# 54 of 66 gate/up pairs as seven block products of 256 tokens each

## What is computed

```python
h = rms_norm(x, norm_ffn_pre[i])
gu = jnp.einsum('bsd,df->bsf', h, w_gu[i])
f = jnp.einsum('bsf,fd->bsd', jax.nn.silu(gu[..., :D_FF]) * gu[..., D_FF:], w_down[i])
x = x + rms_norm(f, norm_ffn_post[i])
```

## Time and profile before

| | |
|---|---|
| runs (3) | 2337.39 us median, 2334.93 to 2341.15 |
| the profiled execution's span, first to last instruction | 2331.0 us |
| mean granted TensorE clock | 0.986 |
| busy: TensorE, VectorE, ScalarE, GpSimd | 2232.4, 1015.4, 885.3, 1024.3 us |
| matmuls | 14692 |

### The profile page before, as it was taken

One profiled execution on the slowest core, in us unless ns is written; L12 is line 12 of the kernel. 1 busy time (PEld: TensorE's weight loads), 2 busy tenths in 40 slices (PEclk: granted clock), 3 DMA queues, 4 the chain that ended last, 5 costly groups with the idle time before them and its releaser, 6 DMA issues.

```text
span 2331.0 us, 36126 instructions
## 1 busy us (share of the span) xinstructions
PE 2232.4 (96%) x14692; PEld 1838.9 (79%) x14692; DVE 1015.4 (44%) x1655; ACT 885.3 (38%) x1506; POOL 1024.3 (44%) x605
## 2 busy tenths in 40 slices
PE   7999999999999999999998999999968999999998
PEld 6867888888986688888886888867757778888888
DVE  6264522211346654222116798726674455322212
ACT  5264532322424654323225222353535445322322
POOL 4423544444543155444446444433430465444443
PEclk9999999999999999999999999999989999999999
DMA  6601343333352023333333333332201432333332
GB/s 176 150 25 37 90 118 93 98 101 100 79 127 73 2 64 100 100 93 95 107 86 109 103 100 93 111 100 78 82 3 40 146 84 79 109 97 93 94 99 70
DMA packets 386295, 209.88 MB, mean 90 GB/s; under 512 B 36927, under 2 KB 378663, under 8 KB 385875
## 3 DMA queue, kind: packets, MB, share of 16 engines
q1 hardware_dynamic: 383011, 196.68, 29.7%
q0 software_dynamic: 2448, 9.70, 1.1%
q10 hardware_dynamic: 672, 1.18, 0.1%
HBM read 196.65 MB, written 12.41 MB: 90 GB/s over the span
## 4 chain that ended last, share of the span: by engine, by line
PE 81%; issue 7%; POOL 6%; DVE 4%; ACT 2%; DMA 0%; ACTq 0%; POOLq 0%; DVEq 0%
PE ps L2372 23%; PE ps L2374 23%; PE ps L2373 23%; POOL w_lo L835 3%; PE ps L2582 2%; PE ps L2567 2%; PE ps L2557 2%; POOL x_res L902 1%; PE ps L2545 1%; POOL u_b L932 0%; PE ps L2952 0%; PE ps L2835 0%; PE ps L2946 0%; PE ps L2445 0%; POOL scratch_z L943 0%
## 5 line engine op out<-in xcount | busy, mean ns | idle before, releaser
L835 POOL TENSOR_TENSOR w_lo<-raw,w_hi 128x1024 fp32r<-128x1024 f32 (+2 forms) x344 | 822.8, 2396 | 886.4 <-ACT w_hi L1026 881.4
L2372 PE MATMUL ps<-h_hi,w_hi 128*128 128x512 f32 (+1 forms) x2112 | 816.6, 387 | 22.2 <-DVE h_lo L1714 4.5
L2373 PE MATMUL ps<-h_hi,w_lo 128*128 128x512 f32 (+1 forms) x2112 | 804.7, 381 | 0.0
L2374 PE MATMUL ps<-h_lo,w_hi 128*128 128x512 f32 (+1 forms) x2112 | 804.6, 381 | 0.0
L1026 ACT ACTIVATE w_hi<-raw 128x1024 fp32r<-128x1024 f32 (+1 forms) x344 | 358.1, 1042 | 1111.9 <-PE ps L2374 1100.1
L2372 PEld LDWEIGHTS ps<-h_hi,w_hi 128*128 128x128 f32 x2112 | 399.0, 189 | 114.9 <-issue 32.6
L2374 PEld LDWEIGHTS ps<-h_lo,w_hi 128*128 128x128 f32 x2112 | 399.1, 189 | 76.6
L2373 PEld LDWEIGHTS ps<-h_hi,w_lo 128*128 128x128 f32 x2112 | 399.4, 189 | 74.8 <-issue 1.2
L2372 PE MATMUL ps<-hid_hi,w_hi 128*128 128x512 f32 (+1 forms) x616 | 221.8, 360 | 0.0
L2374 PE MATMUL ps<-hid_lo,w_hi 128*128 128x512 f32 (+1 forms) x616 | 220.9, 359 | 0.0
L2373 PE MATMUL ps<-hid_hi,w_lo 128*128 128x512 f32 (+1 forms) x616 | 220.9, 359 | 0.0
(11 more groups left out here) (360 smaller groups left out, 2457.8 us busy)
## 6 DMA issues: line engine op xcount, KB each, us to landing
raw<-in_w_gu SPq DMA_DIRECT2D x88, 512.0 KB, 3.7
raw<-in_w_in SPq DMA_DIRECT2D x56, 512.0 KB, 3.7
raw<-in_w_down SPq DMA_DIRECT2D x32, 448.0 KB, 3.5
raw<-in_ffn_w_gate SPq DMA_DIRECT2D x22, 512.0 KB, 3.7
raw<-in_ffn_w_up SPq DMA_DIRECT2D x22, 512.0 KB, 3.7
raw<-in_w_in_b SPq DMA_DIRECT2D x20, 512.0 KB, 3.7
raw<-in_w_down SPq DMA_DIRECT2D x16, 512.0 KB, 3.7
raw<-in_w_out SPq DMA_DIRECT2D x16, 512.0 KB, 3.8
```

The costliest lines, as they stand in the source:

```text
L835: nc.gpsimd.tensor_tensor(lo[:, k0:, :], src[:, k0:, :], hi[:, k0:, :].bitcast(f32), ALU.subtract).then_inc(lo_done, 1)
L2372: nc.tensor.matmul(bank, wh[:, k, :], ah[:, part], start=first, stop=False)
L2373: nc.tensor.matmul(bank, wl[:, k, :], ah[:, part], start=False, stop=False)
L2374: return nc.tensor.matmul(bank, wh[:, k, :], al[:, part], start=False, stop=end)
```

## The change

Pairs 0, 1, 2 and 21 stay as they are (CLASSIC). The other 18 pairs (SEVEN) of each FFN are computed by a block scheme. Take the gate and the up as two rows, the inputs as two halves of four chunks and the tokens as two halves of 256: a product of 2x2 blocks by 2x2 blocks. It has eight block products of 4 chunks x 256 tokens; the new form has seven. For these the kernel forms
- of the activations, once per FFN, four sums of 4 chunks x 256 tokens (`t_sum`, VectorE, `gated_sums`, eight instructions inside the joint and eight behind the first gate), each with a high part by ScalarE (`t_hi`) and a low part (`t_lo`, two by VectorE, two by GpSimd); `later_left` holds one scaled quarter (ScalarE);
- of the weights, per pair, S1, S2 and S4 by VectorE into two PSUM banks (`w_sums`, `w_last_sum`), with high parts by ScalarE and low parts by VectorE (`low_of_sum`), and S3 by GpSimd (`w_diff`). The plain quarters A11, A12 and A22 are split by ScalarE and GpSimd (`high_part`, `low_parts`).

TensorE does the products in the order A11, A12, S2, S1, S3, S4, A22, each 4 chunks x 3 matmuls of 256 tokens, and accumulates several into one bank. What a bank holds in between is copied by ScalarE (`kept`) and added by VectorE: C11, C22, C12 in the code are the results gate/first half, up/second half, gate/second half, and C21 is up/first half. The `w_hi` and `w_lo` slots are now handed out by half slots, and `used` counts pieces. `hid` is kept whole for all 22 tiles; the high and low parts of tiles 3 to 21 come after the last block product, apart from three. Some semaphores are merged with others. The cut diff, its indentation of twelve shortened:

```diff
+HALF = TOK // 2
+CLASSIC = (0, 1, 2, KF - 1)
+SEVEN = tuple(f for f in range(KF) if f not in CLASSIC)
+A11, A12, S2, S1, S3, S4, A22 = range(7)
+T_OF = {S1: 0, S2: 1, S3: 2, A22: 3}
...
+def low_parts(p):
+    s = seven_at[p]
+    diff = w_diff[:, s % 2, :, :]
...
+    nc.gpsimd.tensor_tensor(diff, raw[:, raw_slot[p], 0:4, :], raw[:, raw_slot[p + 1], 0:4, :], ALU.subtract
+                            ).then_inc(sg["w_by_pool"], 1)
+    for j, src in ((A11, raw[:, raw_slot[p], 0:4, :]), (A12, raw[:, raw_slot[p], 4:8, :]), (S3, diff),
+                   (A22, raw[:, raw_slot[p + 1], 4:8, :])):
+        pool.wait_ge(hi_done, place_of[p, j] + 1)
+        pool.wait_ge(used, split_after[p, j])
+        nc.gpsimd.tensor_tensor(split_of(w_lo, p, j), src, split_of(w_hi, p, j).bitcast(f32), ALU.subtract
+                                ).then_inc(lo_done, 1)
...
+def gated_lows(tag):
+    split_lo(L["gu" + tag].p0 + 4)
+    pool.wait_ge(sg["t_steps"], 18 * int(tag) + 8)
+    split_lo(L["gu" + tag].p0 + 5)
+    for m, i in enumerate((T_OF[S3], T_OF[A22])):
+        pool.wait_ge(sg["t_by_act"], 8 * int(tag) + 7 + m)
+        nc.gpsimd.tensor_tensor(t_lo[:, i, :, :], t_sum[:, i, :, :], t_hi[:, i, :, :].bitcast(f32), ALU.subtract
+                                ).then_inc(sg["t_low_by_pool"], 1)
+    split_lo(L["gu" + tag].p1)
...
+def high_part(p, j):
+    s = seven_at[p]
...
+    act.wait_ge(used, split_after[p, j])
+    nc.scalar.activation(split_of(w_hi, p, j), src, ACT.Copy).then_inc(hi_done, 1)
+    if j == A22:
+        nxt[0] += 2
...
+    if after in ("gu0", "gu1", "gu2"):
+        for c in range(4):
+            nc.scalar.activation(beside_x(name, later_left[:, c, :]), x_part(name, c, cols_of(1)), ACT.Copy,
+                                 scale=gain(c)).then_inc(sg["t_by_act"], 1)
...
 def ffn(tag):
-    for i, b in groups("gu" + tag):
-        f = i // 2
...
+    for i in range(4):
+        act.wait_ge(sg["t_steps"], 18 * no + 4 * (i + 1))
+        k = (T_OF[S1], T_OF[S2], T_OF[S3], T_OF[A22])[i]
+        nc.scalar.activation(t_hi[:, k, :, :], t_sum[:, k, :, :], ACT.Copy).then_inc(sg["t_by_act"], 1)
+    first = l.p0 + 2 * SEVEN[0]
+    ahead = {2: (A11, A12), 3: (S2, S1), 4: (S3, S4), 5: (A22,)}
+    last = l.p0 + 2 * SEVEN[-1]
+    for i in range(6):
+        split_hi(min(l.p0 + i + 3, first))
+        act.wait_ge(used, upto(l.p0 + i + 1))
         if i % 2 == 0:
-            n["ffn"] += 1
-            freed(act, L["gu" + tag].g0 + i)
-            nc.scalar.activation(silu[:, f % 2, :], silu[:, f % 2, :], ACT.Silu).then_inc(sg["silu_ready"], 1)
-            if i == 0:
-                split_hi(L["gu" + tag].p0 + 6)
-        else:
-            act.wait_ge(sg["hid_ready"], n["ffn"])
-            nc.scalar.activation(hid_hi[:, f, :], hid[:, f % 2, :], ACT.Copy).then_inc(sg["hid_hi_ready"], 1)
+            freed(act, l.g0 + i)
+            silu_of(i // 2)
+        split_hi(min(l.p0 + i + 4, first))
+        for j in ahead.get(i, ()):
+            high_part(first, j)
+        if i % 2:
+            hid_high(i // 2)
+    high_part(first + 2, A11)
+    for f in SEVEN:
+        p = l.p0 + 2 * f
+        s = seven_at[p]
+        x, y, z, _ = seven_banks(no, s)
+        for j in range(PRODUCTS):
+            if j == A11:
+                keep(0, p, j, x, C11)
+            if j == S2:
+                keep(1, p, j, x, C12)
+            if j == S1:
+                keep(2, p, j, z, C22)
+            if j == A22:
+                gated_to(act, s, GATE)
+                silu_of(f)
+            if j != A22 and p != last:
+                high_part(p + 2, j + 1)
+            if j == A22 and p + 2 < last:
+                high_part(p + 4, A11)
+            if p == last and j in (S1, A22):
+                split_hi(p + 3 + (j == A22))
+    for f in range(3, 6):
+        hid_high(f)
+    act.wait_ge(used, place_of[last, A22] + 1)
+    split_hi(l.p1 + 1)
+    for f in range(6, 10):
+        hid_high(f)
+    split_hi(l.p1 + 2)
+    freed(act, l.g0 + 6)
+    silu_of(KF - 1)
+    for f in range(10, KF):
+        hid_high(f)
+    n["hid"] += KF
...
+def gated_sums(no, name, gain, second):
+    def left(c, half):
+        return x_part(name, c, cols_of(half))
+    def t_of(j, c):
+        return beside_x(name, t_sum[:, T_OF[j], c, :])
+    for c in () if second else range(4):
+        dve.wait_ge(sg["t_by_act"], 8 * no + c + 1)
+        nc.vector.scalar_tensor_tensor(t_of(S1, c), left(c, 0), gain(c), beside_x(name, later_left[:, c, :]),
+                                       ALU.mult, ALU.subtract).then_inc(sg["t_steps"], 1)
...
+    def w_sums(p):
+        s = seven_at[p]
+        a, b = (chunks(bank) for bank in sum_banks(p))
+        if p == l.p0 + 2 * SEVEN[0]:
+            freed(dve, l.g0 + 2)
+            freed(dve, l.g0 + 3)
+        else:
+            weights_to(dve, s - 1, LOW_S4)
+        nc.vector.scalar_tensor_tensor(a, raw_half(p + 1, 0), -1.0, raw_half(p + 1, 1), ALU.mult, ALU.subtract
+                                       ).then_inc(sg["w_by_dve"], 1)
+        weights_to(dve, s, SUM_S1)
+        nc.vector.scalar_tensor_tensor(b, a, -1.0, raw_half(p, 0), ALU.mult, ALU.subtract
+                                       ).then_inc(sg["w_by_dve"], 1)
+    def low_of_sum(p, j):
+        bank = sum_banks(p)[j == S2]
+        dve.wait_ge(hi_done, place_of[p, j] + 1)
+        dve.wait_ge(used, split_after[p, j])
+        nc.vector.tensor_tensor(split_of(w_lo, p, j), chunks(bank), split_of(w_hi, p, j).bitcast(f32), ALU.subtract
+                                ).then_inc(sg["w_by_dve"], 1)
+    def w_last_sum(p):
+        s = seven_at[p]
+        a, b = (chunks(bank) for bank in sum_banks(p))
+        weights_to(dve, s, LOW_S1)
+        nc.vector.tensor_tensor(a, raw_half(p, 1), b, ALU.subtract).then_inc(sg["w_by_dve"], 1)
...
+    def gated(f):
+        s = seven_at[l.p0 + 2 * f]
+        x, _, _, later = seven_banks(no, s)
+        g = silu[:, f % 2, :]
+        dve.wait_ge(sg["silu_ready"], n["gate"])
+        nc.vector.tensor_tensor(g, g, row, ALU.mult).then_inc(sg["gated"], 1)
+        dve.wait_ge(used, place_of[l.p0 + 2 * f, A22] + 1)
+        gated_to(dve, s, SCALED)
+        nc.vector.tensor_tensor(hid[:, f, 0:HALF], ps[:, x, 0:HALF], g[:, 0:HALF], ALU.mult).then_inc(sg["gated"], 1)
+        nc.vector.tensor_tensor(hid[:, f, HALF:TOK], ps[:, later, 0:HALF], g[:, HALF:TOK], ALU.mult
+                                ).then_inc(sg["hid_ready"], 1)
+    first = l.p0 + 2 * SEVEN[0]
+    classic_gate(0, 0)
+    gated_sums(no, post[0], gain, True)
+    classic_up(0, 1)
+    t_low(S1, 1)
+    t_low(S2, 2)
+    classic_gate(1, 2)
+    classic_up(1, 3)
+    w_sums(first)
+    classic_gate(2, 4)
+    low_of_sum(first, S2)
+    low_of_sum(first, S1)
+    w_last_sum(first)
+    classic_up(2, 5)
+    low_of_sum(first, S4)
+    for f in SEVEN:
+        p = l.p0 + 2 * f
+        s = seven_at[p]
+        x, y, z, later = seven_banks(no, s)
+        g = silu[:, f % 2, :]
+        more = f != SEVEN[-1]
+        if f != SEVEN[0]:
+            gated(f - 1)
+        if more:
+            w_sums(p + 2)
+        dve.wait_ge(used, place_of[p, A12] + 1)
+        dve.wait_ge(sg["kept"], 3 * s + kept_order[A11])
+        nc.vector.tensor_tensor(g[:, 0:HALF], ps[:, y, 0:HALF], kept[:, 0, :], ALU.add).then_inc(sg["gated"], 1)
+        if more:
+            low_of_sum(p + 2, S2)
+            low_of_sum(p + 2, S1)
+            w_last_sum(p + 2)
+        dve.wait_ge(used, place_of[p, S3] + 1)
+        dve.wait_ge(sg["kept"], 3 * s + kept_order[S1])
+        dve.wait_ge(sg["hid_ready"], n["hid"] + f)
+        nc.vector.tensor_tensor(ps[:, later, 0:HALF], ps[:, x, 0:HALF], kept[:, 2, :], ALU.add).then_inc(sg["gated"], 1)
+        if more:
+            low_of_sum(p + 2, S4)
+        dve.wait_ge(used, place_of[p, S4] + 1)
+        dve.wait_ge(sg["kept"], 3 * s + kept_order[S2])
+        nc.vector.tensor_tensor(g[:, HALF:TOK], ps[:, z, 0:HALF], kept[:, 1, :], ALU.add).then_inc(sg["gated"], 1)
+        gated_to(dve, s, C12)
+        nc.vector.tensor_tensor(g, g, row, ALU.mult).then_inc(sg["gated"], 1)
+        n["gate"] += 1
+        if 4 <= f < 7:
+            hid_low(f - 4)
+    gated(SEVEN[-1])
+    for f in range(3, 8):
+        hid_low(f)
+    classic_gate(KF - 1, 6)
+    for f in range(8, 13):
+        hid_low(f)
+    classic_up(KF - 1, 7)
+    for f in range(13, KF):
+        hid_low(f)
...
+def seven_products(no):
+    l = L["gu%d" % no]
+    right = {A11: 0, A12: 4, S4: 4}
+    for f in SEVEN:
+        p = l.p0 + 2 * f
+        s = seven_at[p]
+        x, y, z, _ = seven_banks(no, s)
+        bank_of = {A11: x, A12: y, S2: x, S1: z, S3: x, S4: z, A22: x}
...
+        for j in range(PRODUCTS):
+            if f >= SEVEN[2] and j == A11:
+                gated_to(pe, s - 2, C21)
+            if f >= SEVEN[1] and j == A12:
+                gated_to(pe, s - 1, C11)
+            if j == S1:
+                if f == SEVEN[0]:
+                    freed(pe, l.g0 + 4)
```

(28 more changed lines are left out.)

294 lines of the change are left out of this document (220 added, 74 removed).

## The result

| | before | changed |
|---|---|---|
| median of 20 runs each | 2338.82 us | 2344.84 us |
| lowest to highest | 2332.07 to 2344.07 | 2339.88 to 2348.22 |
| profiled span | 2331.0 | 2342.2 |
| mean granted clock | 0.986 | 0.974 |

The ratio is 1.0026, 95% interval 1.0017 to 1.0034: 6.0 us slower, which is within 0.3%. The forecast was 2343.0 us, 5.9 us slower. The two profiled spans differ by more, 11.2 us: a device time lies 1.8 us above its execution's span in every execution on record that has both, so the profiled execution of the kernel before (2331.0) was one of its fastest, and a typical one would span about 2337.

What follows compares the result with a forecast made beforehand. TensorE, busy 96% of the span, was taken as the bound. -43.2 (matmuls) + 31.4 (sixth panel) + 6 (clock) + 5.7 (pairs) + 6 (down) = +5.9 on 2337.4, giving 2343 us; range 2323 to 2359.

Steps and rivals of the forecast that it cites:

- TensorE's gain: Gate/up pairs: 84 matmuls of 0.120 us replace 48 of 0.2267, so 10.88 becomes 10.08 us; 54 pairs, -43.2 us.
- The sixth panel: Up panel of pair 2: TensorE waits for its late high and low parts, 9.7 + 12 + 9.7 = +31.4 us.
- the bound of 7 without GpSimd: Lower bound of the sixth panel's wait, 7 us, if GpSimd is not in VectorE's way.
- The clock: TensorE's lower clock after the sixth panel's waits: 1.5 to 3 us each, three times 2, +6 us.
- two sources: Bases for the clock loss: 6 us at the lower level after a 16.2 us wait; 3 of 5 us at program start.
- The pairs: Steady block pairs: nothing lost in 14 of 18, 1.9 us per FFN in the others, +5.7 us; bounds 0 and +16.
- The hid low parts: Pairs 4 to 6: one more low part (0.695 us) in VectorE's ring, costing perhaps 0.5 us each.
- The play of "0.4 us": Slack per pair between the VectorE-ScalarE dependency ring, some 9.7 us with hand-overs, and TensorE's pitch of about 10.
- The rival in which the ring becomes the bound: Steady pairs limited by the VectorE-ScalarE ring at 10.4 us: +16 against 5.7 counted, 2354 us; chance 0.3.
- Down: Down's third panel, behind ScalarE's last hid high part, comes 2 us late: +6 in all, bounds 0 and +9.
- The joint: Stretch before the FFN: eight more VectorE sums and four ScalarE copies fall in idle time; nothing counted.
- the faster rival: VectorE and GpSimd interleave kindly: waits of 7, 9 and 7, no loss in pairs or down; 2322 us, chance 0.13.

Runs made afterwards that it cites:

- x1: The change with GpSimd making the sixth panel's low part ahead of its two t_lo: 2346.6 us, 1.0041 of the kernel before.
- x2: The change with the sixth panel's high part ahead of ScalarE's third t_hi and its low part ahead of GpSimd's t_lo: 2347.2 us, 1.0042 of the kernel before.
- x3: x2 with the first block pair's A11 and A12 high and low parts made early too: 2346.6 us, 1.0044 of the kernel before.
- x7: The change with one more 0.7 us VectorE instruction, result unused, in 13 of 18 block pairs per FFN: 2350.1 us, one execution, no ratio.
- x4: The change with ScalarE making the high part of down's third panel ahead of its last twelve hid_hi: 2350.1 us, 1.0056 of the kernel before.
- x8: The change itself, unaltered, measured again: 2345.8 us, 1.0033 of the kernel before.
- x5: The change with the entry into the block products ordered anew on all four engines: 2338.8 us, 1.0004 of the kernel before.
- x9: x5 plus hid 3 to 5 in pairs 7 to 9, kept A11 ahead of hid 1, third gate earlier: 2323.5 us, 0.9940 of the kernel before.
- x10: x9 with GpSimd waiting for all sixteen activation sums, not twelve, before its first weight difference: 2318.7 us, 0.9923 of the kernel before.
- x11: x10 with the first block pair's A22 high part ahead of the high part of hid 1: 2324.8 us, 0.9956 of the kernel before.

## Why the forecast was right

**TensorE's gain** was exact: the pitch of a steady pair is 10.08 us in all three FFNs, as 84 x 0.120 says. By the rule of the Trainium skill (TensorE: Matmul & The Clock Gate, "Back-to-back issue gap"), which is given there for an isolated matmul, it would be 9.17; no row shows it, and the measurement decides.

**The sixth panel** was the step that mattered: a wait of 8.9, 11.4 and 8.9 where 9.7, 12 and 9.7 were reckoned, by the chain that was written down, with the product in GpSimd's way at 2.01 us. x1 shows GpSimd's share, 1.3 and 2.2 us; the bound of 7 without GpSimd was a little low (7.6). What x2 and x3 add is that the other gates behind this one were as late. For the time of the change this made no difference; for the remedy it made all of it.

**The clock** behind the sixth panel was near what was reckoned: 6 against 6.7, between 1.7 and 2.7 a time. Of its two sources the one long wait was the nearer to the first FFN.

**The pairs**: 5.7 reckoned, 3.8 measured. The first pair loses 0.34 us in each FFN (0.4 was reckoned). The hid low parts cost 0.4, 0.8 and 1.6 us in the three FFNs, and not 1.5 in each; the waits stand at S3 of pairs 5 to 7, one pair behind the low part. This term was mis-sized. One reason is in the rows: VectorE's wait of 0.70 for the silu, into which the `hid_lo` falls. The play of "0.4 us" had no firm ground: the pair's VectorE work adds up to 7.8 us, and with three or four shares of 0.59 the ring is 9.5 or 10.1, not "about 9.2". x7 shows that 0.7 us has room at one place. The rival in which the ring becomes the bound, given 0.3, rested on that number and deserved less.

**Down**: 2 us late was reckoned, 2.33 came, three times. That the clock falls behind so short a wait was not in the sum, 3.2 us. That ScalarE's order is the whole cause was wrong too (x4): VectorE's low parts are as late.

**The joint** costs nearly nothing, as forecast: TensorE's last 30 us ahead of the token scales are as long as before in the first and third FFN, and 0.2 us longer in the second (0.6 in x8).

Smaller slips of the forecast change nothing: two low parts in 5.21 are 2.6 each and not 2.4 (the pair came out at 5.01), and the faster rival's time is 2322, where the range begins at 2323.

So the sum came out within 0.1 us of the medians' difference by luck of the terms: 49.1 us given back were reckoned, 51.3 are in the profile's stages, and the medians show 6.0 and, in the second measurement, 7.8.

## What to carry to other kernels

A change that takes work from the bounding engine is paid for where the others must first fill its new pipeline; read the order of all queues there, and expect several gates to be late together, so that freeing one shows next to nothing (x2, x3) and only the whole entry does (x5, x9, x10). The same block products cost 0.3% with the first order and save 0.8% with another (x10, which also makes three of the hid parts earlier). And a releaser named in a profile is to be held against what the waiting instruction needs, by counting products from the last known point, before a run is spent on it (x11).

## What the hardware showed that I had not expected

- **The clock fell behind a wait of 2.33 us** in down in 15 of 21 cases (seven profiles with that wait, three FFNs each), and in none of three behind waits of 1.22 and 1.56 us with 1 us of matmuls between them (x4). Behind the entry's waits of 4.4 us and more the first matmul was always at the lower level; behind shorter ones both occur: 0.36 us behind 2.98 and 3.18, 0.55 behind 2.96 and 3.05. Where it began at the full level, the clock fell within the next 2 us (mean 0.87 and 0.61).
- **Four 256-wide sums from SBUF took 1.67 us alone and 4.78 beside GpSimd**; GpSimd's two low parts took 5.0 us in the change and 6.2 in x10, beside more of VectorE's. One wait constant moved the delay from one to the other.
